# Values of six decoding samples loaded from ScalarE's queue instead of SyncE's

## What is computed

```python
ka = jnp.concatenate([_gather_pages(pool_a_k, page_table), k_a], axis=1)
va = jnp.concatenate([_gather_pages(pool_a_v, page_table), v_a], axis=1)
kb = jnp.concatenate([_gather_pages(pool_b_k, page_table), k_b], axis=1)
vb = jnp.concatenate([_gather_pages(pool_b_v, page_table), v_b], axis=1)
...
o_a = _diff_attn(q_a, ka, va, q_pos, k_pos, slopes, lam)
o_b = _forgetting_attn(q_b, kb, vb, F_new, F_k, q_pos, k_pos)
```

## Time and profile before

| | |
|---|---|
| three timed runs | 2879.81, 2880.18, 2873.84 us; median 2879.81 us |
| the profiled execution, its own time | 2875.88 us |
| its span | 2874.3 us |
| TensorE matmul, busy | 2648.5 us, 92% of the span |
| TensorE weight loads, busy | 2019.9 us, 70% |
| VectorE, busy | 1558.4 us, 54% |
| ScalarE, busy | 964.0 us, 34% |
| GpSimd, busy | 201.8 us, 7% |
| sample stage | from about 2290 to 2425 us of the span |
| mean granted TensorE clock | 0.958 of full |

### The profile page before, as it was taken

How to read it: one execution, slowest core, us unless ns; L and a number is a source line. 1 busy time by engine, 2 the same in 40 slices (tenths; PEclk the granted TensorE clock), 3 DMA queues, 4 the chain that set the end, 5 groups by cost and what they waited for, 6 DMA issues and landing times. The chain is left out here.

```text
span 2874.3 us, 34640 instructions
## 1 busy us (share of the span) xinstructions
PE 2648.5 (92%) x12711; PEld 2019.9 (70%) x12711; DVE 1558.4 (54%) x2454; ACT 964.0 (34%) x1546; POOL 201.8 (7%) x184
## 2 busy tenths in 40 slices
PE   6699999995899999999999799989999876899998
PEld 1488888884577767777777577767777653688886
DVE  3412214654436545666777277767777644555553
ACT  0411112224212225776000177764444322322221
POOL 4000000221002220000000110000000000000000
PEclk9699999996899999999999899999999988899999
DMA  5545455533445347664443766634546197343431
GB/s 212 192 154 223 166 179 172 177 94 108 156 141 165 115 138 175 150 157 113 123 119 98 170 130 143 145 81 86 116 85 132 37 327 264 137 132 131 132 123 55
DMA packets 285136, 413.46 MB, mean 144 GB/s; under 512 B 78411, under 2 KB 169675, under 8 KB 275501
## 3 DMA queue, kind: packets, MB, share of 16 engines
q1 hardware_dynamic: 281314, 383.23, 47.2%
q10 hardware_dynamic: 2626, 28.26, 2.6%
q0 software_dynamic: 1056, 0.13, 0.1%
HBM read 274.03 MB, written 137.52 MB: 143 GB/s over the span
## 5 line engine op out<-in xcount | busy, mean ns | idle before, releaser
L1260 DVE TENSOR_REDUCE max_neg_top<-max_s_ps 128x1 f32<-128x1024 f32 (+7 forms) x384 | 349.0, 913 | 170.8 <-PE max_s_ps L1318 115.6
L467 PE MATMUL proj_z<-proj_w_hi,h_hi 128*128 128x512 f32 x768 | 302.0, 393 | 0.0
L467 PE MATMUL proj_z<-proj_w_hi,h_lo 128*128 128x512 f32 x768 | 299.3, 390 | 0.0
L467 PE MATMUL proj_z<-proj_w_lo,h_hi 128*128 128x512 f32 x768 | 298.9, 389 | 0.0
L1634 ACT ACTIVATE att_b_pf<-att_b_s_ps 128x1024 f32<-128x1024 f32 (+2 forms) x160 | 141.0, 899 | 144.5 <-PE att_b_s_ps L1688 77.3
L1227 ACT ACTIVATE max_s_ps<-max_s_ps,max_neg_top 128x128 f32<-128x128 f32 (+2 forms) x192 | 161.0, 838 | 72.0 <-DVE max_neg_top L1260 71.5
L1342 PE MATMUL max_z<-gate_w_hi,h_hi 128*128 128x512 f32 (+1 forms) x432 | 178.0, 412 | 4.5 <-PEq L670 4.5
L1451 ACT ACTIVATE att_a_pf<-att_a_s_ps,head_bias 128x1024 f32<-128x1024 f32 (+3 forms) x160 | 158.2, 989 | 58.9 <-PE att_a_s_ps L1528 31.6
L1342 PE MATMUL max_z<-gate_w_lo,h_hi 128*128 128x512 f32 (+1 forms) x432 | 177.5, 411 | 0.0
L1342 PE MATMUL max_z<-gate_w_hi,h_lo 128*128 128x512 f32 (+1 forms) x432 | 176.5, 409 | 0.0
L467 PE MATMUL proj_z<-gate_w_hi,h_hi 128*128 128x512 f32 (+1 forms) x432 | 173.5, 402 | 0.0
(11 more groups left out here) (339 smaller groups left out, 5723.8 us busy)
## 6 DMA issues: line engine op xcount, KB each, us to landing
proj_w_raw<-in_w_in SPq DMA_DIRECT2D x144, 256.0 KB, 4.6
mrg_mix<-scratch_mixes SPq DMA_DIRECT2D x16, 1024.0 KB, 4.8
ada_w<-in_w_ada SPq DMA_DIRECT2D x8, 1536.0 KB, 10.1
scratch_w_split<-proj_w_hi ACTq DMA_DIRECT2D x6, 2048.0 KB, 6.7
scratch_w_split<-proj_w_lo ACTq DMA_DIRECT2D x6, 2048.0 KB, 13.2
gate_w_hi<-scratch_w_split SPq DMA_DIRECT2D x48, 256.0 KB, 3.9
gate_w_lo<-scratch_w_split SPq DMA_DIRECT2D x48, 256.0 KB, 4.1
map_qm<-scratch_q_hi SPq DMA_DIRECT2D x48, 256.0 KB
```

Source lines behind the costliest of these rows:

```text
L467: ins = nc.tensor.matmul(out, left(*lt), right(*rt), start=first and n == 0, stop=last and n == len(terms) - 1)
L1260: nc.vector.tensor_reduce(neg_top[:, kh, u, qt:qt + 1], s_ps[:, x % SLOTS, 0:width[x]], AX.X, ALU.max, negate=True).then_inc(max_done, 1)
```

## The change

SyncE keeps all keys, the values of samples 0 and 1, and the slices of output weights. The values of samples 2 to 7 are loaded by ScalarE: in each of its bodies 1 to 6, right after the exponential for sample b + 1 and ahead of the high part of the weights' slice, it waits for `pv_done` of at least b, reads 4 page numbers into registers and issues 8 DMAs. The wait on `const_in` on both sides of it has long been met. On SyncE, keys and slices now alternate in one loop, so that the keys of each sample from 3 on stand behind the wait for the slice that follows the previous keys.

```diff
+        def load(eng, b, s, what):
+            pages = [eng.value_load(k.pages[0:1, ds(b * NPG + g, 1)], min_val=0, max_val=NPOOL - 1) for g in range(NPG)]
+            for n in (2 * what, 2 * what + 1):
+                for g in range(NPG):
+                    eng.dma_start(kv[s][n][:, g:g + 1, :], caches[n][ds(pages[g], 1)].rearrange("n r c -> r n c")).then_inc(kv_in[s][n], 16)
...
-                def next_k(b, s):
+                def next_k(b, s, i):
                     sp.wait_ge(S["filled"], 1)
                     sp.wait_ge(S["turned"], b * 8 - 8)
-                    load(b, s, 0)
-
-                def next_v(b, s, i):
-                    sp.wait_ge(S["filled"], 1)
-                    sp.wait_ge(S["pv_done"], b - 1)
-                    load(b, s, 1)
+                    load(sp, b, s, 0)
                     sp.wait_ge(k.out_w.lo_done[s], i)
                     load_out_w(k, sp, i, s)
 
-                load(0, 0, 0)
-                load(1, 1, 0)
-                load(0, 0, 1)
-                load(1, 1, 1)
+                for what in range(2):
+                    for s in range(2):
+                        load(sp, s, s, what)
                 for s in range(2):
                     load_out_w(k, sp, 0, s)
-                next_k(2, 0)
-                with sp.Fori(1, TURNS - 1) as i:
-                    next_k(i * 2 + 1, 1)
-                    next_v(i * 2, 0, i)
-                    next_k(i * 2 + 2, 0)
-                    next_v(i * 2 + 1, 1, i)
-                next_k(NB - 1, 1)
-                next_v(NB - 2, 0, TURNS - 1)
-                next_v(NB - 1, 1, TURNS - 1)
+                with sp.Fori(1, TURNS) as i:
+                    for s in range(2):
+                        next_k(i * 2 + s, s, i)
...
                     if not last:
                         k_turned(b + 1)
                         probabilities(b + 1)
+                    if not first and not last:
+                        act.wait_ge(S["const_in"], 16)
+                        act.wait_ge(S["pv_done"], b)
+                        act.wait_ge(S["const_in"], 16)
+                        load(act, b + 1, 1 - s, 1)
                     out_w_high(k, act, i, s)
```

## The result

The changed kernel takes **2921.72 us** (median of 4 runs, 2917.91 to 2923.21) where the kernel before takes 2877.34 (median of 4). The ratio is 1.0153, 95% interval 1.0135 to 1.0170: slower, by 44.4 us. The profiled execution took 2922.34 us, its span is 2920.8, its mean granted clock 0.952 (before: 2875.88, 2874.3, 0.958).

The account below looks back on a forecast made before the run. TensorE, 92% busy, bounds the whole kernel, but the sample stage is bound by a ring of waits among TensorE, VectorE and ScalarE. 35.1 + 7.6 + 0.8 = 43.5 us gives 2919.4 to 2923.3; predicted 2921 us, range 2905 to 2938.

Parts of the forecast that it names:

- ScalarE's queue stands at the exponential's wait: On ScalarE, the load begins only with the exponential, not in the 4.74 us of idling before it.
- 5.85 us per load, 35.1 for six: The slice starts 6.6 us after the exponential instead of 0.75, lengthening the ring by 5.85 us per load.
- The reads' 2.5: Four register reads on ScalarE's queue cost 2.5 us per load, SyncE's price rather than GpSimd's 4.3.
- The rival of dearer issue: ScalarE's reads cost like GpSimd's, first issues are slow, or keys are late: 2926 to 2936 us, chance 0.12.
- The clock, +7.6 in bodies 2 to 6 and +0.8 in body 7: TensorE's clock slows behind 7.2 us idling ahead of turn_p: 2.2 us per body, less 3.4 already there; about 0.8 in body 7.
- the rival in which it holds: TensorE's clock does not fall behind the longer hole ahead of turn_p: 2908 to 2920 us, chance 0.13.
- The keys' wait unchanged: TensorE's 6.62 us wait for keys 2 in body 1 stays, as keys 2 keep their place on SyncE.
- Keys behind the slices, counted 0: On SyncE, keys issued later behind the slice's wait still land in time, with 2.4 us of cover.
- Nobody waited for SyncE, so removing six loads gains 0: Taking six value loads off SyncE, each about 2.5 us reads and 3.8 us issuing, counts 0.
- the cover: Time between the keys' landing and TensorE wanting them: 2.4 us, or 0.2 if the clock does not fall.
- the slow ring: Closed chain of waits among TensorE, VectorE and ScalarE in each body, including the slice, lengthened by 5.85 us per load.

Follow-up runs that it names:

- e2: Changed kernel with the waits and value load still on ScalarE but moved ahead of the exponential: 2894.98 us, 1.0064 of the kernel before.
- e4: Changed kernel with the 4 register reads of every ScalarE load done twice: 2938.3 us, 1.0221 of the kernel before.
- e6: Changed kernel with 56 unused identity transposes on TensorE ahead of turn_p in bodies 2 to 7: 2912.75 us, 1.0137 of the kernel before.
- e3: Changed kernel with the waits and value load moved behind ScalarE's weight slice: 2900.85 us, 1.0088 of the kernel before.
- f2: Kernel before, with the slice's high part ahead of the exponential and low part ahead of the biased scores: 2873.92 us, 0.9992 of the kernel before.
- e1: Changed kernel with values 2 to 7 issued by GpSimd instead of ScalarE, SyncE's order kept: 2879.71 us, 1.0024 of the kernel before.
- g1: Kernel before, with values 2 to 7 on GpSimd, keys 2 early, slice parts out of the ring, slices behind keys: 2864.74 us, 0.9963.
- f3: Kernel before, with keys 2 issued early and both slice parts moved out of the ring: 2873.83 us, 0.9995 of the kernel before.
- f1: Kernel before, with keys 2 issued ahead of values 1 and the slices on SyncE: 2874.16 us, 0.9997 of the kernel before.
- e5: Changed kernel with 40 unused identity transposes on TensorE ahead of turn_p in every body but the first: 2919.58 us, 1.0157 of the kernel before.
- h1: Kernel before, with keys 2 early, slice parts out of the ring, page numbers computed instead of read (other pages attended): 2854.49 us, 0.9922.

## Why the prediction held, point by point

**The forecast of 2921 us met 2921.7.** The mechanism was right; that the number fits to 1 us is luck, since two terms were too small and a third, which the sum did not have, made up for them. Its steps:

- *ScalarE's queue stands at the exponential's wait.* Shown: the load starts behind the exponential in each of the six bodies, and its 4.74 to 5.54 us of idling are untouched. e2 adds that the idling can be used, by an order written by hand and not by the queue running ahead. The rule of the Trainium skill ("Perfetto Trace Analysis", DVE / Act engine instruction) is for a wait that is pushed along with its instruction. Here the wait is an instruction of its own or, in the loop, is compared with a register, and in none of the six bodies did the load start ahead of it. No run had a plain wait carried by the exponential, so what such a one would do here stays open.
- *5.85 us per load, 35.1 for six.* Measured: the slice comes 6.66 us behind the exponential in the body shown, 6.51 to 6.77 in all six, less 0.75: 35.2 in sum. The reads' 2.5, taken from SyncE and not from GpSimd, is borne out by e4 (2.1 to 2.4). In e6 the term stands alone: 29.5 for five where it says 29.3. The rival of dearer issue is excluded: four reads took 2.3 us, and ScalarE's issues 339 to 402 ns each.
- *The clock, +7.6 in bodies 2 to 6 and +0.8 in body 7.* The mechanism was right: the window's clock fell to 0.79, and the rival in which it holds is excluded. The size was too small. Bodies 2 to 6 grew by 38.68, of which 29.5 are holes and 9.2 slower work, and e6 gives 9.15 by filling the holes. From turn_p to their end the five bodies took 11.4 to 13.0 us, 1.9 to 3.5 over the 9.48 at full clock and 2.5 on average, where 2.2 was taken. Body 7, up to the merge's first activation, grew by 7.97 where 6.65 was summed.
- *The keys' wait unchanged.* 6.77 against 6.62. But the body behind it took 12.62 us where it took 15.65: the clock came back earlier (0.88 against 0.70), with nothing in its own instructions changed. This -3.0 has no term in the prediction, and it is what made two undersized terms come out at the right sum. The other traces do not tie it to the change. Body 1 took 12.62 us in e3, 12.66 in e4 and 12.95 in e6, but 15.44 in e2, where its instructions are the same and the load stands on ScalarE too; and it took 12.94 in f2, whose SyncE order is that of the kernel before. Both lengths occur behind a wait of 6.0 to 7.1 us, and why was not tried. The windows of body 1 in e2, then in e3:

  ```profile
  2333.84:2349.28 15.44, 15.44 (x106) 0.71 0.73 239
  ```

  ```profile
  2332.27:2344.89 12.62, 12.62 (x107) 0.88 0.67 227
  ```

- *Keys behind the slices, counted 0.* They landed in time in all of bodies 2 to 6. With A the end of body 2, 2366.82, the low part ends at A + 8.2 (2373.82 + 1.22; predicted 8.15), SyncE's first key issue is at 2378.40, A + 11.6 (12.25 by the prediction's terms), and the keys are wanted at 2387.57, A + 20.75 (predicted 20.9). e1 shows the other half of the sentence: the cover was the slow ring itself, and goes with it.
- *Nobody waited for SyncE, so removing six loads gains 0.* The 0 was right, and the reason was incomplete. SyncE was full and ahead. Its relief was worth nothing in the changed kernel, whose ring is slower, and nothing in e1 either, whose ring is that of before (there the keys stand behind the slices). With the ring shortened and the values off SyncE it is worth 9 us in g1 (f3 at 0.9995 of before, g1 at 0.9963), the new place of the slices included.

SyncE's rows in the changed kernel show the relief. From keys to keys it now takes 20.5 us (2357.92 to 2378.40) and 21.1 (2378.40 to 2399.50), with long idling between:

```profile
2378.40 1.89 SPq L1928 DMA_DIRECT2D smp_k_a<-in_cache_a_k  x4
2380.39 1.80 SPq L1928 DMA_DIRECT2D smp_k_b<-in_cache_b_k  x4
2395.72 0.33 SPq L1867 DMA_DIRECT2D wo_raw<-in_w_out_b  x1
```

**Where expectations failed.** f1, f2 and f3 expected gains from removing a wait that stood in the profile. Another came in its place: the first slice's landing in f1, late loads in f2, both in f3. e2's holes were as expected, but the slower work behind them had no term; e3's were smaller, and the late values at the end had none. e5 expected a hole filled for the most part to keep the clock up, and with 2.8 to 3.3 us of idling left it fell all the same. e6 expected 12 to 16 us and got 9. g1's expectation rested on transfers at their limit, and they moved a fifth more (389 against 320 to 329 GB/s); its rival, 12 us less, is what came. h1 gained 22 us where 8 to 14 were expected.

**What stays open.** Why body 1's clock recovers early in some executions and late in others; where e1's 0.24% lies; what limits transfers at 389 GB/s; and what of g1's gain comes from each of its parts, since it was run only as a whole. g1 still has a hole of 6.25 us in body 1, for the first slice.

## What to carry to other kernels

A DMA issue and the register reads ahead of it are work of the engine whose queue they stand on: price them (here 6.3 to 6.5 us per 4 reads and 8 transfers) and put them where that engine idles, which is before its awaited instruction and not behind it. Even there they were not free here (e2, 0.64% slower). Before a load is moved off a queue because "nobody waits for it", compare that queue's period with the loop's: if it is full and only ahead, it is the next bound, and it pays to relieve it once the loop is shorter. A removed wait is worth the distance to the next one, so name that one first; two removed one by one for nothing may be worth something together with a third.

## What the hardware showed that was not expected

- Issuing is not of constant price. ScalarE's first four issues of a load took 339 to 378 ns each in the changed kernel and up to 1572 ns in e2, where SyncE had just issued 8 transfers of 256 KB; in h1 four issues on SyncE took up to 4.16 us. This was seen beside many transfers under way each time, but no run varied their number alone.
- The DMA share was 0.95 to 0.97 at 327 to 329 GB/s in the kernel before, and 1.04 to 1.05 at 389 in g1 and h1. A share near 1 did not mean that no more could be moved.
- In e5, the stretch of TensorE behind 40 dense transpositions and 3.14 us of idling began at full clock (turn_p in 1.10 us) and then fell (keys in 3.44 against 1.97). The first work behind a hole does not tell what the clock will be for the next.
